# Two transformer blocks in f32 parts on one Trainium2 core: paired weight tiles at each start, weight pieces split one further ahead, output tiles begun inside attention 2

## The reference

```python
h  = modulate(rms_norm_2(x, g_mix[l]), sa, ca)
hc = modulate(rms_norm_2(ctx, g_mix[l]), sa_c, ca_c)
u, q, k, v = split_heads(h @ w_in[l])          # 512 columns each
uc, qc, kc, vc = split_heads(hc @ w_in[l])
q, k = apply_rope(q, cos, sin), apply_rope(k, cos, sin)
o_att = diff_attn_blocks(q, concat(kc, k), concat(vc, v), lam)
mix = concat([pool_mixer(u, w_pool[l], s_pool[l]), head_out(o_att, g_subln[l], lam_init)])
x = x + ga * (mix @ w_out[l])
x = x + gm * sq_relu_mlp(modulate(rms_norm_2(x, g_mlp[l]), sm, cm), w_mlp1[l], w_mlp2[l])
# if not last: the same for ctx, whose queries attend to the context alone
```

## Time and profile before

| | before |
|---|---|
| time, median of 3 runs | 2936.38 us (2931.28 to 2939.44) |
| time of the profiled execution | 2934.72 us |
| its span | 2932.9 us |
| mean granted clock of PE | 0.967 |
| instructions | 48482 |
| chain that ended last | PE 86%, DVE 8%, issue 2%, DMA 2%, ACT 1% |

### The profile page before, as it was taken

One profiled execution on the slowest core, in us unless ns is written; L12 is line 12 of the kernel. 1 busy time (PEld: TensorE's weight loads), 2 busy tenths in 40 slices (PEclk: granted clock), 3 DMA queues, 4 the chain that ended last, 5 costly groups with the idle time before them and its releaser, 6 DMA issues.

```text
span 2932.9 us, 48482 instructions
## 1 busy us (share of the span) xinstructions
PE 2720.2 (93%) x20932; PEld 2170.7 (74%) x20932; DVE 1441.0 (49%) x2470; ACT 888.3 (30%) x1508; POOL 88.3 (3%) x141
## 2 busy tenths in 40 slices
PE   6899888888899999997989899999999889899998
PEld 4677566668788788885867678888888666688876
DVE  3455455668843544445356653333334456544434
ACT  3444411110132333323235432222132335333322
POOL 0000011111200000000000000000000000000000
PEclk9999999899899999998999999999999999999999
DMA  6100546540023132221000211111110100222220
GB/s 253 58 29 11 192 178 227 193 149 4 4 108 116 72 115 87 90 107 58 29 30 30 87 58 58 58 58 68 76 58 29 40 29 29 115 98 103 86 86 29
DMA packets 17954, 242.43 MB, mean 83 GB/s; under 512 B 2032, under 2 KB 2192, under 8 KB 2896
## 3 DMA queue, kind: packets, MB, share of 16 engines
q1 hardware_dynamic: 16416, 231.94, 21.2%
q0 software_dynamic: 1328, 7.39, 0.6%
HBM read 237.23 MB, written 2.10 MB: 82 GB/s over the span
## 4 chain that ended last, share of the span: by engine, by line
PE 86%; DVE 8%; issue 2%; DMA 2%; ACT 1%; DVEq 0%; ACTq 0%; SPq 0%
PE ps L333 57%; PE ps L1256 7%; PE ps L395 2%; PE ps L1815 2%; PE ps L2034 2%; PE ps L910 1%; DMA raw<-in_w_ada 1%; PE ps L2062 1%; PE ps L2078 1%; PE ps L866 1%; DVE hh L486 1%; PE ps L2080 1%; PE ps L2079 1%; PE ps L912 1%; PE ps L911 1%
## 5 line engine op out<-in xcount | busy, mean ns | idle before, releaser
L333 PE MATMUL ps<-hh,ws 128*128 128x512 f32 x3600 | 855.5, 397 | 32.4 <-DVE hh L486 26.0
L333 PEld LDWEIGHTS ps<-hh,ws 128*128 128x128 f32 x3600 | 678.6, 190 | 192.4 <-issue 39.7
L324 DVE TENSOR_TENSOR ws<-raw,ws 128x1024 fp32r<-128x1024 f32 x295 | 360.9, 1224 | 236.3 <-ACT ws L316 236.2
L316 ACT ACTIVATE ws<-raw 128x1024 fp32r<-128x1024 f32 x295 | 309.4, 1050 | 506.5 <-PE ps L333 433.2
L333 PE MATMUL ps<-g,ws 128*128 128x512 f32 x1536 | 364.5, 395 | 0.0
L333 PEld LDWEIGHTS ps<-g,ws 128*128 128x128 f32 x1536 | 286.1, 188 | 67.2
L1256 PEld LDWEIGHTS ps<-ar 64*64 64x64 f32 x6656 | 215.6, 141 | 55.8 <-issue 36.9
L1256 PE MATMUL ps<-ar 64*64 64x64 f32 x6656 | 231.1, 227 | 19.7 <-issue 10.8
L1569 DVE SCALAR_TENSOR_TENSOR xT<-ps,mods,xT 128x512 f32<-128x512 f32 x120 | 90.1, 751 | 323.3 <-PE ps L333 323.3
L333 PE MATMUL ps<-gg,ws 128*128 128x512 f32 x960 | 226.1, 395 | 0.0
L333 PEld LDWEIGHTS ps<-gg,ws 128*128 128x128 f32 x960 | 180.3, 188 | 43.7
(11 more groups left out here) (320 smaller groups left out, 3000.5 us busy)
## 6 DMA issues: line engine op xcount, KB each, us to landing
raw<-in_w_ada SPq DMA_DIRECT2D x36, 2048.0 KB, 8.6
raw<-in_w_m SPq DMA_DIRECT2D x32, 2048.0 KB, 7.8
raw<-in_w_mlp SPq DMA_DIRECT2D x16, 2048.0 KB, 7.7
raw<-in_w_in SPq DMA_DIRECT2D x8, 2048.0 KB, 7.6
raw<-in_w_mg SPq DMA_DIRECT2D x8, 1536.0 KB, 6.7
raw<-in_w_out SPq DMA_DIRECT2D x6, 2048.0 KB, 7.8
raw<-in_w SPq DMA_DIRECT2D x5, 2048.0 KB, 7.8
xT<-in_xT POOLq DMA_DIRECT2D x1, 2048.0 KB, 16.8
```

What stands on the lines that cost most here:

```text
L316: e.activation(w_of(n)[0], pieces[n][2], ACT.Copy).then_inc(*hi(n))
L324: e.tensor_tensor(l, pieces[n][2], h.bitcast(F32), ALU.subtract).then_inc(*lo(n))
L333: m = e.matmul(o, a, b, start=n == 0, stop=n == 3 * kt - 1)
```

## The change

- A new helper `pe_tiles` does two weight tiles k by k, so that six matmuls stand behind each k of hh. It is used for tiles 0 and 1 of m0, m1 and m2 and in the head of a layer; the two pieces are marked used together.
- w_in's tiles are in another order: a (u3, k0, q0, k1), b unchanged, c (q3, u2, u1, u0). In in2, x's parts of u3 and k0 come together, then x's of q0, then (layer 0) the context's statistics, then the context's parts of u3, k0 and q0, turn k0, v, turn q0, k1, the pool of u3, q1, turn k1.
- ACT and DVE split the pieces of u3, k0 and q0 at the start of the head, and the piece of k3 at the end of in2.
- The flows end with u2, u1, u0 (windows of 8, 4 and 2 positions).
- The first out tile's first six k's (in the order of `OK`) are done in attention 2, right before its last norm product, and tile 1's behind it; the last two k's of both are interleaved.
- In attention 1 each score waits for its own q's turn.

The diff, cut to its core:

```diff
             a = comes(f"{tag}a", w[0], 4096)
-            columns(f"{tag}a", a, [(0, (l, "u", 0))])
+            columns(f"{tag}a", a, [(0, (l, "u", 3)), (1, (l, "k", 0)), (2, (l, "q", 0))])
             slot2[l] = hold(f"mix{l}")
             dense(f"{tag}v", w[3], pk=2, pc=512)
-            columns(f"{tag}a", a, [(1, (l, "k", 0)), (2, (l, "q", 0)), (3, (l, "k", 1))])
+            columns(f"{tag}a", a, [(3, (l, "k", 1))])
             b = comes(f"{tag}b", w[1], 4096)
             columns(f"{tag}b", b, [(0, (l, "q", 1)), (1, (l, "k", 2)), (2, (l, "q", 2)), (3, (l, "k", 3))])
             soft2[l] = hold(f"att{l}")
             c = comes(f"{tag}c", w[2], 4096)
-            columns(f"{tag}c", c, [(0, (l, "q", 3)), (1, (l, "u", 1)), (2, (l, "u", 2)), (3, (l, "u", 3))])
+            columns(f"{tag}c", c, [(0, (l, "q", 3)), (1, (l, "u", 2)), (2, (l, "u", 1)), (3, (l, "u", 0))])
...
+
+        def pe_tiles(e, ns, names, rhs, w, order, ready):
+
+            lhs = [pe_piece(e, n) for n in ns]
+            for name in names:
+                for t in ps.take(name):
+                    e.wait_ge(*t)
+            for i, k in order:
+                e.wait_ge(*dve[ready, k])
+                (lh, ll), (rh, rl) = lhs[i](k), rhs(k)
+                o = ps[names[i]][:, 0:w]
+                e.matmul(o, lh, rh, start=k == 0, stop=False)
+                e.matmul(o, lh, rl, start=False, stop=False)
+                m = e.matmul(o, ll, rh, start=False, stop=k == KT - 1)
+                if k == KT - 1:
+                    m.then_inc(*acc(names[i]))
+
+        by_feature = [(i, k) for k in range(KT) for i in range(2)]
...
             qb, t4, p = items[i]
             sl = halves(p)
             q = qa[sl, t4, qb * 128:qb * 128 + 128]
+            e.wait_ge(*dve[("q", t4), "end"])
...
         def tensor_attention(e):
             banks = cycle((5, 6, 7))
             e.wait_ge(*dve["mb"])
-            e.wait_ge(*dve[("q", 3), "end"])
             for i, parts, _ in attention_steps():
...
             def tensor(e, ready):
+                for j, h, hid, x, w, bufs, bank in rows_:
+                    n = start("u", 0)
+                    pe_tiles(e, [n, n + 1], [(tag, "u", 0, m, j) for m in range(2)], of(h), w, by_feature, ready[j])
+                for m in range(2):
+                    acc.also(("used", start("u", 0) + m))
                 for q in range(4):
                     for m in range(8):
-                        pe_tile(e, start("u", q) + m, [((tag, "u", q, m, j), of(h), w, ready[j] if m + q == 0 else None)
+                        if m + 8 * q < 2:
+                            continue
+                        pe_tile(e, start("u", q) + m, [((tag, "u", q, m, j), of(h), w, None)
                                                        for j, h, hid, x, w, bufs, bank in rows_])
                     for m in range(8):
...
-            flows = [(name, m, j) for name, m in (("k", 2), ("q", 2), ("k", 3), ("q", 3), ("u", 1), ("u", 2), ("u", 3))
+            flows = [(name, m, j) for name, m in (("k", 2), ("q", 2), ("k", 3), ("q", 3), ("u", 2), ("u", 1), ("u", 0))
...
                 e.wait_ge(*dve[l, "lam"])
                 e.matmul(ps[l, "lam"][:, 0:2], ones[:, :], l2, start=True, stop=True).then_inc(*acc((l, "lam")))
-                if l == 0:
-                    pe_stat(e, cs, TC, rms_bufs(TC))
 
             def scalar_head(e):
+                split_hi(e, tile_piece[l, "u", 3] + 2)
...
             def vector_head(e):
+                split_lo(e, tile_piece[l, "u", 3] + 2)
...
             def tensor_in2(e):
-                groups = both_streams("u", 0)
-                pe_tile(e, tile_piece[l, "u", 0], [x[0:3] + (t,) for x, t in zip(groups, (tx, tc))])
+                n = tile_piece[l, "u", 3]
+                pe_tiles(e, [n, n + 1], [(l, "u", 3, 0), (l, "k", 0, 0)], of(hh), T, by_feature, tx)
+                pe_tiles(e, [n + 2], [(l, "q", 0, 0)], of(hh), T, [(0, k) for k in range(KT)], tx)
+                if l == 0:
+                    pe_stat(e, cs, TC, rms_bufs(TC))
+                for i, (name, m) in enumerate((("u", 3), ("k", 0), ("q", 0))):
+                    if name == "k" or not last:
+                        pe_tiles(e, [n + i], [(l, name, m, 1)], of(hc2), TC, [(0, k) for k in range(KT)], tc)
+                    acc.also(("used", n + i))
+                pe_turn(e, "k", 0)
...
-                for i, (name, m) in enumerate(ahead):
-                    pe_tile(e, tile_piece[l, name, m], both_streams(name, m))
-                    if i:
-                        pe_turn(e, *ahead[i - 1])
-                    else:
-                        e.wait_ge(*come["wpl"][l])
-                        for j in streams_of("u"):
-                            pe_pool(e, 0, j)
+                pe_turn(e, "q", 0)
+                pe_tile(e, tile_piece[l, "k", 1], both_streams("k", 1))
+                e.wait_ge(*come["wpl"][l])
+                for j in streams_of("u"):
+                    pe_pool(e, 3, j)
+                pe_tile(e, tile_piece[l, "q", 1], both_streams("q", 1))
+                pe_turn(e, "k", 1)
...
             def scalar_in2(e):
-                n = tile_piece[l, "u", 0]
-                split_hi(e, n + 2)
-                for j in streams_of("u"):
-                    act_up(e, 0, j)
-                split_hi(e, n + 6)
+                n = tile_piece[l, "u", 3]
+                act_up(e, 3, 0)
+                act_keep(e, "k", 0, 0)
+                act_keep(e, "q", 0, 0)
+                if not last:
+                    act_up(e, 3, 1)
+                split_hi(e, n + 3)
+                act_keep(e, "k", 0, 1)
+                split_hi(e, n + 4)
+                if not last:
+                    act_keep(e, "q", 0, 1)
+                split_hi(e, n + 7)
                 for i in range(6):
                     e.wait_ge(*acc[l, "v", i])
                     e.activation(vall[:, i, :], ps[l, "v", i], ACT.Copy).then_inc(*act((l, "v", i)))
-                for name, m in ahead:
+                for name, m in ahead[2:]:
                     split_hi(e, tile_piece[l, name, m] + 2)
                     for j in streams_of(name):
                         act_keep(e, name, m, j)
+                split_hi(e, tile_piece[l, "q", 1] + 3)
...
             def vector_in2(e):
-                n = tile_piece[l, "u", 0]
-                split_lo(e, n + 6)
+                n = tile_piece[l, "u", 3]
+                e.wait_ge(*come["rope"][l])
+                dve_turn_sin(e, "k", 0)
+                dve_turn_cos(e, "k", 0)
+                split_lo(e, n + 7)
+                dve_turn_sin(e, "q", 0)
+                dve_turn_cos(e, "q", 0)
                 for j in streams_of("u"):
-                    dve_pool_sums(e, 0, j)
-                    dve_pool_mean(e, 0, j)
-                e.wait_ge(*come["rope"][l])
-                for i, (name, m) in enumerate(ahead):
-                    split_lo(e, tile_piece[l, name, m] + 2)
-                    if i:
-                        dve_turn_sin(e, *ahead[i - 1])
-                        dve_turn_cos(e, *ahead[i - 1])
-                    else:
-                        for j in streams_of("u"):
-                            dve_pool_out(e, 0, j)
+                    dve_pool_sums(e, 3, j)
+                    dve_pool_mean(e, 3, j)
+                split_lo(e, tile_piece[l, "k", 1] + 2)
+                for j in streams_of("u"):
+                    dve_pool_out(e, 3, j)
+                split_lo(e, tile_piece[l, "q", 1] + 2)
+                dve_turn_sin(e, "k", 1)
+                dve_turn_cos(e, "k", 1)
+                split_lo(e, tile_piece[l, "q", 1] + 3)
...
+            OK = [3, 2, 1, 4, 5, 6, 0, 7]
+
+            def pe_out_tiles(e, order):
+
+                n = first[f"o{l}0"]
+                names = [(l, "out", m, 0) for m in range(2)]
+                for i, k in order:
+                    if k == OK[0]:
+                        e.wait_ge(*hi[n + i])
+                        e.wait_ge(*lo[n + i])
+                        for t in ps.take(names[i]):
+                            e.wait_ge(*t)
+                    e.wait_ge(*dve[(l, "mixlo", 0), k])
+                    lh, ll = (x[:, k, :] for x in w_of(n + i))
+                    e.matmul(ps[names[i]], lh, hh[:, 0, k, :], start=k == OK[0], stop=False)
+                    e.matmul(ps[names[i]], lh, hh[:, 1, k, :], start=False, stop=False)
+                    m = e.matmul(ps[names[i]], ll, hh[:, 0, k, :], start=False, stop=k == OK[-1])
+                    if k == OK[-1]:
+                        m.then_inc(*acc(names[i]))
...
                     for x in at("product"):
+                        if x == ("norm", 3, 0 if last else 1):
+                            ps.use = range(8 - len(out_rows))
+                            pe_out_tiles(e, [(0, k) for k in OK[0:6]])
                         pe_product2(e, *x)
...
             def tensor_out2(e):
-                ps.use = range(8 - len(out_rows))
```

(21 more changed lines are left out.)

2 lines of the change are left out of this document (1 added, 1 removed).

## The result

The changed kernel takes **2905.74 us** (median of 4 runs, 2901.58 to 2908.0) against 2936.24 us (4 runs) of the kernel before: ratio 0.9896, 95% interval 0.9878 to 0.9914, so 25 to 36 us less. A second measurement gave 2902.92 us, ratio 0.9888 (0.9864 to 0.9911). The forecast was 2904.

What follows compares the result with a forecast made beforehand. PE, busy 93% of the span, bounds the kernel; only its idle stretches and the lower clock behind them can shrink. Terms sum to 32.1 us off the profiled 2934.72, so 2902.6, median 2904; range 2893 to 2917.

Steps and rivals of the forecast that it cites:

- k3 split early: Attention 2: waits for w_in's third block and the slow clock behind go; 9.8 us gained in layer 0, 10.5 in layer 1.
- 0.475: Clock cost, derived from the v group: 0.475 us lost for each us at the lower clock level.
- Head of layer 0: Head and in2, layer 0: x fills PE's idle, less a new wait before v; 0.8 us gained (-4 to +4).
- Head of layer 1: Head and in2, layer 1: a 5.6 us wait becomes 3.6, slow start filled; 3.6 us gained (1 to 5).
- Pairs: MLP starts: tiles 0 and 1 together are not paced by DVE; m0 0.9, m1 3.6, m2 0.9 us gained.
- End of attention 2: Layer 0: fewer last DVE sums, out matmuls fill a wait, 2.7 us gained; layer 1: norm starts later, -0.7.
- Attention 1: Start of attention 1: PE's first wait, 6.0 us on the cast, stays; 0 gained.
- The slow rival: Clock does not return in v after the new 3.6 us idle, in both layers; 2961 us, chance 0.03.

Runs made afterwards that it cites:

- k3_undone: The undone run: the changed kernel without the early split of k3's piece; 2925.35 us, ratio 0.9959 to the kernel before.
- k3_alone: The kernel before with one edit only, k3's piece split at the end of in2; 2918.23 us, ratio 0.993.
- before_again: The kernel before, run again unchanged as a control; 2937.18 us, ratio 0.9999.
- masks_early: The changed kernel with attention 1's three mask casts on DVE in front of the last convolution instead of behind it; 2903.43 us, ratio 0.9884.
- norm_first: The changed kernel with the last layer's first 18 matmuls of out tile 0 behind the last norm product; 2901.41 us, ratio 0.9881.

## Why the prediction was right, point by point

- **k3 split early** (forecast 9.8 and 10.5): right in mechanism, 8.1 and 11.1 measured by the undone run. At the stall itself the sizes are right too. Matched matmul by matmul, k3_alone is 9.8 us ahead of before from behind the stall of layer 0 on and 10.6 in layer 1; k3_undone is 9.0 and 10.2 behind the changed kernel (its idle stretch of 7.15 has 4.4 us of the lower level behind it, where before has 7.41 and 5.6). The split itself costs 0.3 and 1.1 to 1.2 in front of the stall, where 0.3 and 1.0 were forecast. The difference to 8.1 and 11.1, and to k3_alone's 7.9 and 9.9, comes 100 us and more later, at the end of attention 2, by where the lower level lies there. These are the windows over the same matmuls in layer 0, from a norm product to the first matmuls of the out tiles (us, PE busy, matmuls, granted clock), for before, before_again and k3_alone:

```profile
1635.73:1656.45 20.72, 12.73 (x41) 0.84 0.00 0
1633.51:1654.23 20.72, 15.45 (x40) 0.60 0.00 0
1627.18:1649.88 22.70, 17.43 (x41) 0.55 0.06 12
```

  Before_again has 10 us more of the lower level than before, 2.7 us more of PE's busy time, and the same length: PE waits for DVE and ACT there, and a slower PE only waits less. K3_alone has 4 us more still, which lie in the out tiles, where PE no longer waits, and it is 2.0 longer, which is 0.475 for each. Now the changed kernel, k3_undone and masks_early, over the same matmuls:

```profile
1625.58:1645.56 19.98, 13.89 (x43) 0.74 0.00 0
1632.09:1651.13 19.04, 12.96 (x43) 0.82 0.00 0
1630.51:1648.94 18.43, 12.34 (x42) 0.81 0.00 0
```

  Here out tile 0 is inside, and the 3.4 us more of the lower level that the changed kernel has cost 0.9 and 1.5. The forecast had no term for the clock at this place, and the 0.475, taken from v, where PE never waits, does not hold in every stretch.
- **Head of layer 0** (0.8): 0.9 to 1.3 measured. The sum has a slip of 0.4 (1398.0 + 9.5 is 1407.5, not 1407.1), so by its own rows the term is 0.4. Its parts were right too: idle for hc 2 to 3 forecast and 2.81 measured, wait in front of v 3.6 and 3.35. The clock dipped in front of v (v's first 12 matmuls took 4.59).
- **Head of layer 1** (3.6): 2.4. The mis-sized term is again the clock. I took 4.0 us at the lower level for x and 3.2 for v; the 8 us behind each start have 0.63 and 0.79, which is 5.9 and 3.4:

```profile
2268.35:2276.35 8.00, 8.00 (x23) 0.63 0.04 16
2294.82:2302.82 8.00, 8.00 (x28) 0.79 0.00 0
```

  2.1 us more at 0.475 is 1.0 of the 1.2 that are missing.
- **Pairs** (0.9, 3.6, 0.9): 1.1, 4.8, 1.9. m0 is right. For m1 and m2 the step that failed is that the lower level would last as long as before. Of the ten executions with pairs, m1's lower level ends 3.2 to 3.3 us behind its first matmul in four (the stretch is then 548.5) and 4.6 to 5.7 in six (549.1 to 549.7); without pairs 4.9 to 6.1. m2's ends after 2.8 to 3.2 in eight and 5.9 to 6.1 in two; without pairs 5.0 to 5.8. So the clock comes back early in four of ten executions with pairs at m1 and in eight of ten at m2 (363.2 to 363.4 there, 364.6 and 364.7 in the other two), and in none of the three without; that the denser matmuls do it is not shown. I had weighed the Trainium skill, page "TensorE: Matmul & The Clock Gate", part 1 (a time, not a number of matmuls) and said that the rows speak for it, with a microsecond more for each start otherwise. m1 and m2 gained that microsecond in this trace, m0 did not. The rows of before (4.5 us at the lower level at m0, 6.1 at m1) could not carry what I read from them, and the runs decide neither for a time nor for a number.
- **End of attention 2** (2.7 and -0.7): 4.4 and -0.7 by the undone run against before. Of the 4.4 in layer 0, 0.7 lies at the stall, which is a little shorter there; 3.6 lies behind it, 0.9 more than forecast. PE's idle time in the stretch falls by 3.9 with the stall still there. Which of u's order and the out tiles gave it was not tried apart. That the row of layer 0 met its forecast so closely (12.5 and 12.4) is luck: k3 gave 1.7 less and this term 1.7 more. Layer 1 is right to the tenth, and norm_first shows its mechanism.
- **Attention 1** (0): right, for half of the reason. I took the cast as the last of PE's waits, because the list of waits named it, and it was; but a PSUM bank was free only 0.4 us before it, and the sum did not know of it.
- **What the sum did not have**: 4.9 us more between attention 1 and m0 in the changed kernel's profiled execution, which varies by itself. The terms add up to 32.1, the stretches without that row to 34.0. In the profiled execution that row hid the excess of the others. The medians, 2905.74 and 2902.92, lie on both sides of 2904 and can't tell 32 from 34: that they come within 2 us of it is better than the terms deserve.
- **The slow rival**: the idle in front of v did bring the clock down, and it was back after 3.4 us. The advice of the Trainium skill, page "TensorE: Matmul & The Clock Gate", section on why this matters for kernels, against idle gaps between bursts of matmuls points at something real here: removing that gap gave 11.6 us, 6.7 of it the idle itself and, by 10.4 us less of the lower level, 4.9 the clock.

The mean granted clock rose from 0.967 to 0.972: 2(1-c) of the span is 194 us at the lower level before and 163 after. Plain idle and the clock behind it went together.

## What to carry to other kernels

When a load waits for the last reader of a block, look for the one small instruction that is that reader, and ask whether it can be done before the next phase begins: one piece's split (1.06 us on ACT, 1.22 on DVE), moved forward, was worth 19 of the 34 us that the stretches gained. When a step is moved ahead, look in the same queue for what it now stands in front of (turn k0 before v's split, statistics behind q0, out tile before the last norm): three such swaps gave 20 us more. Cut traces at rows that both kernels have, and compare stretches: most repeat within 0.4 us where totals scatter by 8. And match them instruction by instruction before you price a stall: the length of a stretch mixes it with what the clock does 100 us later.
